# Moving the retention's states, a table warm-up, a GpSimd wait and the routing's counts in a hybrid decoder layer

## The reference

```python
def layer(x, l, p, pos0, kv_past, ret_s0, conv_buf, lru_h0, gla_s0):
    xn = rms_norm(x, p['norm1'])
    aq, ak, av, bq, bk, bv, bg, cx, cg, dq, dk, dv, dr, da = project(xn, p['w_in'])
    ...
    s_ret, ob = chunked(ret_chunk, ret_s0, chunk, pad, qb, kb, vb)
    ob = (group_norm(ob, p['rn']).reshape(b, l_len, BRANCH_W) * jax.nn.silu(bg.astype(F32))).astype(x.dtype)
    ...
    h = rglru(xc, lru_h0, p['lru_wa'], p['lru_ba'], p['lru_wx'], p['lru_bx'], p['lru_lam'])
    ...
    gates = jax.nn.sigmoid(xn @ p['w_merge'] + p['b_merge']).reshape(b, l_len, N_BRANCH, D_MODEL)
    proj = jnp.einsum('blnw,nwd->blnd', br, p['w_branch'])
    hres = x + jnp.sum(gates * proj, axis=2) @ p['w_out']
    y = hres + hier_moe(rms_norm(hres, p['norm2']), p['rg_w'], p['rg_b'], p['re_w'], p['re_b'],
                        p['ex_w1'], p['ex_w3'], p['ex_w2'])

def ret_chunk(s0, q, k, v):
    ...
    o = jnp.einsum('bhtj,bjhv->bthv', a, v)
    o = o + jnp.einsum('bthk,bhkv->bthv', q, s0) * jnp.exp((t[:, None] + 1.0) * lg[None])[None, :, :, None]
    kd = k * jnp.exp((t_len - 1.0 - t)[:, None] * lg[None])[None, :, :, None]
    s = jnp.exp(t_len * lg)[None, :, None, None] * s0 + jnp.einsum('bjhk,bjhv->bhkv', kd, v)
```

## Time and profile before

| | us |
|---|---|
| median of 3 runs | 790.43 (789.67 to 791.04) |
| the profiled execution, its own time | 790.43 |
| its span, first to last instruction | 788.5 |
| PE busy | 762.8 (97% of the span) |
| DVE busy | 382.4 (48%) |
| POOL busy | 294.9 (37%) |
| ACT busy | 225.5 (29%) |

### The profile page before, as it was taken

How to read it: one execution, slowest core, us unless ns; L and a number is a source line. 1 busy time by engine, 2 the same in 40 slices (tenths; PEclk the granted TensorE clock), 3 DMA queues, 4 the chain that set the end, 5 groups by cost and what they waited for, 6 DMA issues and landing times.

```text
span 788.5 us, 14312 instructions
## 1 busy us (share of the span) xinstructions
PE 762.8 (97%) x5277; PEld 545.0 (69%) x5277; DVE 382.4 (48%) x713; ACT 225.5 (29%) x436; POOL 294.9 (37%) x221
## 2 busy tenths in 40 slices
PE   8999999999999999999999999999999799999992
PEld 7887778676677888777767788888888634333330
DVE  4637777677497689543534113734533712031210
ACT  4131344342423454142414223322201512020100
POOL 0000331364553975255524554434250112332314
PEclk9999999999999999999999999999999999999996
DMA  9342662355665542245535453342761899999933
GB/s 363 119 162 82 204 195 86 85 159 168 184 178 188 169 137 66 80 150 175 174 122 174 122 190 141 100 159 69 267 267 51 310 337 410 371 389 370 384 116 50
DMA packets 72538, 148.32 MB, mean 188 GB/s; under 512 B 13335, under 2 KB 47144, under 8 KB 70420
## 3 DMA queue, kind: packets, MB, share of 16 engines
q1 hardware_dynamic: 65716, 135.43, 49.9%
q0 software_dynamic: 5920, 10.82, 5.6%
q10 hardware_dynamic: 832, 1.16, 0.5%
HBM read 137.71 MB, written 18.90 MB: 199 GB/s over the span
## 4 chain that ended last, share of the span: by engine, by line
PE 92%; DMA 3%; ACT 2%; DVE 1%; issue 1%; POOL 0%; SPq 0%; POOLq 0%; ACTq 0%
PE ps L874 23%; PE ps L608 17%; PE ps L1215 11%; PE ps L843 7%; PE ps L1120 6%; PE ps L1285 5%; PE ps L651 3%; PE ps L623 3%; PE ps L900 2%; PE ps L597 2%; PE ps L678 1%; PE ps L1204 1%; DMA scr_x<-cst 1%; PE ps L707 1%; PE ps L694 1%; DMA tmp<-in_xT 1%
## 5 line engine op out<-in xcount | busy, mean ns | idle before, releaser
L608 PE MATMUL ps<-xn,ring 128*128 128x268 f32 (+1 forms) x576 | 136.5, 391 | 0.2 <-ACT qk L1378 0.2
L608 PEld LDWEIGHTS ps<-xn,ring 128*128 128x128 f32 x576 | 106.9, 190 | 24.5 <-issue 4.2
L2576 POOL TENSOR_TENSOR kv<-kv,sgd 128x1024 f32<-128x1024 f32 (+1 forms) x32 | 80.4, 2526 | 98.8 <-DVE tmp L1848 51.7
L1530 ACT ACTIVATE sgt<-sgt,vec 128x260 f32<-128x260 f32 x60 | 30.1, 510 | 122.8 <-DVE sgt L2129 70.8
L2691 POOL DMA_INDIRECT out_y<-cst,gtab x24 | 37.3, 1555 | 70.9 <-DVE cst L2498 42.0
L843 PE MATMUL ps<-br,ring 128*128 128x260 f32 x256 | 61.0, 386 | 0.6 <-DVE sgt L2133 0.6
L874 PE MATMUL ps<-xn,ring 128*128 128x260 f32 x240 | 58.0, 385 | 0.0
L874 PE MATMUL ps<-xn,qb 128*128 128x260 f32 x240 | 57.6, 383 | 0.1
L843 PEld LDWEIGHTS ps<-br,ring 128*128 128x128 f32 x256 | 47.8, 190 | 11.2 <-issue 3.2
L1876 DVE TENSOR_REDUCE sgd<-kv 128x32 f32<-128x1024 f32 (+1 forms) x32 | 40.7, 1279 | 21.4 <-POOL kv L2576 21.4
L874 PEld LDWEIGHTS ps<-xn,qb 128*128 128x128 f32 x240 | 45.4, 190 | 7.4 <-issue 0.4
(11 more groups left out here) (525 smaller groups left out, 1499.6 us busy)
## 6 DMA issues: line engine op xcount, KB each, us to landing
ring<-in_w_mg SPq DMA_DIRECT2D x32, 640.0 KB, 4.7
kv<-in_kc SPq DMA_DIRECT2D x128, 128.0 KB, 2.3
kv<-in_vc SPq DMA_DIRECT2D x128, 128.0 KB, 2.1
ring<-in_w_in SPq DMA_DIRECT2D x24, 512.0 KB, 5.0
kv<-in_w SPq DMA_DIRECT2D x8, 1024.0 KB, 13.1
br<-in_w SPq DMA_DIRECT2D x7, 1024.0 KB, 12.9
sgd<-in_w SPq DMA_DIRECT2D x6, 1024.0 KB, 14.4
qk<-in_w SPq DMA_DIRECT2D x6, 1024.0 KB, 11.0
```

Of the source, the lines that this page charges most:

```text
L608: mm = pe.matmul(ps[:, 2 * (t % 2) + h, 0:hw], wsl(c, k), xnv[:, k, col0 + h * hw:col0 + (h + 1) * hw], start=(k == 0), stop=(k == KT - 1))
L1530: act.activation(g, g, ACT.Sigmoid, bias=vv(V_BM + 8 * "ABCD".index(n) + m + i)).then_inc(g_a, 1)
L2576: pool.tensor_tensor(kb, kb, qbc[:, b:b + 1, :].to_broadcast([P, HALF // 2 + (half and u), 256]), ALU.mult)\
```

## The change

It has five parts, one or two on each engine.

1. POOL: unit 1 of the keys no longer waits for rot_ok. The store of `ret_p` moves from before unit 28 to before unit 26, ahead of the store of `c`.
2. PE: all retention states are made behind the end of DR1 (they were made half after the first half of GC0, half after GC0). The samples move from behind GC0 into the middle of DA. ACT's two copies move with them, the states' copy before DA's copy, the samples' copy behind it. The counting of the two pairs of semaphores is swapped to suit.
3. ACT: the one-element sigmoid that brings the table in moves from ahead of DK's copy to ahead of CR0's.
4. DVE: the memset of vtok, with its wait for st_ev, moves ahead of the BMEAN subtractions, and one sum of keys (`sampled`) changes sides.
5. Routing: the subtraction r[0] is made right after the maximum; on ACT both exponentials move up among the copies of rows; the counts of tokens per expert come from one matmul of 80 columns and a reduction on DVE in place of five matmuls of 16 columns, and one semaphore serves rank and count. The work from the counts moves ahead of the positions.

The diff, cut to its core:

```diff
...
+        ecnt, eov, eend, edel = [view(dr, 400 + 16 * i, NE) for i in range(4)]
...
-        kt_t, ro_mm, st_mm = [(ret_t, i + 1) for i in range(3)]
-        (kd_ok, rs_ok), (b_raw, st_ev) = [[(e, i + 1) for i in range(2)] for e in (ret_v, ret_a)]
+        kt_t, st_mm, ro_mm = [(ret_t, i + 1) for i in range(3)]
+        (kd_ok, rs_ok), (st_ev, b_raw) = [[(e, i + 1) for i in range(2)] for e in (ret_v, ret_a)]
...
-            def ret_states(heads):
+            def ret_states():
...
-                for h in heads:
+                for h in range(H):
...
-                if (name, end) == ("GC0", 0):
-                    ret_states(range(2))
+                if (name, end) == ("DR1", 1):
+                    ret_states()
+                if (name, end) == ("DA", 0):
+                    ret_samples()
...
-                gate_tile("C", m, beside)
+                gate_tile("C", m)
                 if m == 0:
-                    ret_samples()
-                    ret_states(range(2, H))
                     pe.wait_ge(br_ok, 1)
...
-            mm.then_inc(rank_ok[0], 1)
-            for b in range(NB):
-                mm = pe.matmul(ps[:, 5, 0:NE], every, selm[:, b, :], start=(b == 0), stop=(b == NB - 1))
-            mm.then_inc(cnt_ok[0], 1)
+            pe.matmul(ps[:, 5, 0:NB * NE], every, selm, start=True, stop=True).then_inc(rank_ok[0], 1)
...
                     act.activation(drv, drv, ACT.Silu)
+                    act.wait_ge(*st_mm)
+                    act.activation(rst, ps[0:64, 7, 0:256].rearrange("p (h v) -> p h v", h=H), ACT.Copy).then_inc(st_ev[0], 1)
+                if (name, end) == ("DA", 1):
+                    act.wait_ge(*ro_mm)
+                    act.activation(brv[:, 2:4, SEQ:N], ps[:, 6, 0:2 * DEC].rearrange("p (t b) -> p t b", t=2), ACT.Copy)\
+                       .then_inc(b_raw[0], 1)
...
                 elif name == "DK":
-                    act.activation(sc[:, 54:55], eps, ACT.Sigmoid)
                     copy(name, dkv, HT)
...
                 elif name == "CR0":
                     act.wait_ge(par, 2)
+                    act.activation(sc[:, 54:55], eps, ACT.Sigmoid)
                     copy(name, aa[:, 0, :], HT, ACT.Sigmoid, bias=vv(V_BA))
...
-            act.wait_ge(r1, 1)
-            for b in range(NB):
+            def normed(b):
                 act.wait_ge(tt_t, b + 1)
                 bk = (0, 2, 6)[b % 3]
                 act.activation(fold(tk[b], 512), ps[0:RB, bk:bk + 2, :], ACT.Copy, scale=sc[0:RB, 40 + b:41 + b]).then_inc(tt_a, 1)
+
             act.wait_ge(r1, 2)
             act.activation(rt[0:RB, 0, :, :], rt[0:RB, 0, :, :], ACT.Exp).then_inc(r2, 1)
+            for b in range(2):
+                normed(b)
             act.wait_ge(r1, 3)
...
+            for b in range(2, NB):
+                normed(b)
...
-            at_k = sampled(at_k, 2)
+            dve.wait_ge(*st_ev)
+            dve.wait_ge(s_v, 16)
+            dve.wait_ge(kv_out, 48)
+            dve.memset(vtok[:, 0:2048], 0.0)
+            at_k = sampled(at_k, K_TAIL)
+
             for t in range(2):
                 dve.wait_ge(pj, AT[f"BMEAN{t}"] + 1)
...
             link(dve.tensor_reduce(one[2], gl, X, ALU.max))
+            tt(r[0], gl, one[2].to_broadcast([RB, NB, 4]), ALU.subtract).then_inc(r1, 1)
             link(tt(r[3], gl, one[2].to_broadcast([RB, NB, 4]), ALU.is_equal))
...
+            link(dve.tensor_reduce(ecnt, ps[:, 5, 0:NB * NE].rearrange("p (b e) -> p e b", b=NB), X, ALU.add))
...
-            dve.wait_ge(*cnt_ok)
...
                 if x < K_CONV:
                     pool.wait_ge(scomb, K_STEP[x])
-                if x == 1:
-                    pool.wait_ge(rot_ok, 2)
...
                     pool.dma_start(o["ret_s"], rs0).then_inc(rs_out, 16)
+                    pool.wait_ge(*st_ev)
+                    pool.dma_start(o["ret_p"], rst).then_inc(rst_out, 16)
                     pool.wait_ge(c_out, 1)
...
-                if x == K_LAST + 2:
-                    pool.wait_ge(*st_ev)
-                    pool.dma_start(o["ret_p"], rst).then_inc(rst_out, 16)
```

35 lines of the change are left out of this document (11 added, 24 removed).

## The result

The kernel before: 790.92 us (median of 18 runs, 788.38 to 792.44). The changed kernel: 795.06 us (median of 18 runs, 792.09 to 802.93). The ratio of the runs is 1.0065, with a 95% interval of 1.0045 to 1.0087. So it is slower. The medians differ by 4.1 us, where the prediction had 4.0; by the ratio it is 5.1.

The account below looks back on a forecast made before the run. PE was taken as the bound up to 610 us, a chain of waits in routing. 2.2 + 0.4 + 1.35 + 0.2 = 4.15 on 790.43 gave 794.6, stated as 794.4 for possible overlap; range 791.9 to 796.0.

Parts of the forecast that it names:

- term 1: Attention, step 2: POOL's earlier second key multiply delays DVE's rotate(1), so PE waits; +2.2 us (0 to 2.4).
- 0.1 us of slack: Attention, step 3: PE's transposes needing combine(2) follow its scores with 0.1 us to spare, so the delay reaches PE nearly whole.
- Term 2: Sigmoid table load behind ACT's copy of DK: the copy of CR0 and PE's CI0 come later; +0.4 us (0.3 to 0.5).
- the dearer switch: Sigmoid warm-up on ACT: a table switch costs more than its load, about 1.4 us more, 795.8 us; chance 0.04.
- Term 3: Retention states right behind DR1: PE waits for DVE's kd_ok, no longer hidden by other work; +1.35 us (0 to 1.6).
- Term 4: Routing: later index table delays the gather slightly, the later last store costs nothing; +0.2 us (0 to 0.5).
- Rotation undisturbed: Attention: DVE keeps rotate(1)'s three instructions together and POOL comes after, costing 0 there; 792.3 us, chance 0.14.
- Not slower: Before kd_ok and at the rotation: DVE is favoured against POOL, only 0.4 + 0.2 stay; 791.0 us, chance 0.10.
- The stores don't count: Routing: judges the rival that, with the queue not full, rows land up to 3.3 us later; 797.7 us, chance 0.07.

## Where the prediction held, and the step that failed

The forecast was 794.4, slower; the median came to 795.06, inside the range of 791.9 to 796.0. The ratio gives 790.43 x 1.0065 = 795.6, and the plain mean of the 18 runs, 796.3, is above the range. The direction and the four places are right. That the number came so near is luck, since two errors of opposite sign meet in it.

The step that failed is "every microsecond for which PE is made to wait is added to it": a wait was priced at its own length, and what the clock does behind it was put at nothing without a reason. The waits in the first profile, with the routing's 0.19, are 2.6 us in all, where the sum had 4.15; of the 5.1 us by the ratio, the other 2.5 came on top of the waits, as an estimate, and the traces show the lower clock behind them: 1.7 us lost behind the rotation, and 6.7 behind the retention's wait in the profiled run of the upper group. The second step that failed is the size of term 1, below.

- **Term 1, the rotation, 2.2.** On DVE exact: L1855 at 2.75 for 0.72, 2.03 late. On PE it was 0.99, where the sum had 2.2. The step that failed here is "0.1 us of slack": it read the slack off a run in which a hold of 1.1 on L1846 had just used it up. I had that hold in hand, as evidence for the mechanism, and didn't see that it was itself a delay that another run needn't have. What made up for it was the clock: L608 took 1.4 to 1.7 more in four of five traces of the changed kernel (in neither its second profile nor that of the kernel with this part alone). Measured alone the part cost 2.2, but with 0.8 to 3.6 as the interval, and its own trace has 0.98 of waiting near 229 that isn't the part's. The agreement with the predicted 2.2 proves nothing.
- **Term 2, the table, 0.4.** Confirmed by the trace at 0.36, and the dearer switch refuted.
- **Term 3, the states, 1.35.** The wait is there: 1.10, and 0.8 to 1.6 over the five profiles. Behind it PE is 0.91 later in the first (3.90 - 2.99). The missing step is what a wait does to the clock when narrow work follows it. If all 19 upper runs are of that kind, as the one profiled is, it cost 6.1 more in 19 of 66 runs, 1.8 on average, more than the wait itself. None of my rivals held this; the range reached up to 796.0, and all of the upper group is above it. I had noted that the states' work on PE "is the same": its total is, but it now stands in one narrow row of 8 us behind a wait.
- **Term 4, the routing, 0.2.** The gather's release is 4.12 later where 3.93 had come in: 0.19. The store's landing gave way to the table as foreseen. The whole arm, as a part alone, can't be told from zero.
- **The sum.** It was made as if the end of the routing were carried on to the end. There the lower clock happened to fall 1.5 us more cheaply than in the profile of before. That run had such a stretch in it, at 633 to 636, which I had read as a fixed part of the kernel.
- **The rivals.** Rotation undisturbed: no, in every trace without POOL's wait one instruction of it is held for 2. Not slower: a state of kd_ok ready in time occurred in one kernel with the part. The stores don't count: the last one was issued 3.2 later and nothing waited.

What stays open is what exactly decides between the two groups. The longer wait (2.2) brought all five of its runs to the upper group, 1.63 did once, and 1.3 and below did not in four profiles. What makes 1.6 out of 1.1 is open too. A hold of DVE near 223 alone doesn't: L1938 took 3.31 us in the upper run's trace and 1.27 in the first one, where L1937 was held instead, by 0.9; but it took 3.31 in the second and fourth profiles as well, with waits of 1.26 and 1.06. And the high run of the kernel with the rotation alone has no explanation here.

## What to carry to other kernels

Where TensorE is full, price a new wait twice: once as idle time, and once for the work behind it, which may run at 1.2 GHz; a wait ahead of narrow products was the dearest one here, and matmuls into a bank that nobody reads are a cheap test of it. When a row of one profile shows an engine being held, ask whether the slack that you read next to it would still be so small without that hold. And look at the spread of the runs, not only at the median: a group of runs 6 us above the rest was about a third of this change's cost. A difference of 1 us between two single profiles may be neither's: the wait near 228 and the falls of the clock in the routing come and go without any change.

## What the hardware showed that I had not expected

- A wait of 0.99 us of TensorE was followed by some 3 us at half clock in 7 of 9 traces, and, with idle matmuls in the wait, in none of three.
- The clock fell to 1.2 GHz with TensorE busy throughout, behind 6.7 us of products of 64, 16 and one column (0.57 from 247 to 249), and in the order of before as well (0.66 from 255 to 260).
- With narrow work behind a wait of 1.6 to 2.2 us, the lower level held for 14 to 16 us, four times as long as behind the rotation, where wide products followed.
- 1.1 us more of waiting raised a kernel's time by 6 us in all five runs, and 11 matmuls that compute nothing took 5 of them back in all four.
- Every trace has the lower clock for 3 to 7 us around the routing but one (the changed kernel with fillers there too), and where it falls moves: the stretch behind the logits took 175.5 to 178.3 us.
